# One token tile at a time behind the recurrent block, and half of the sparse queries moved into the first gather phase

## The reference, cut to what matters

```python
h = h + gated @ w_out                                   # recurrent block's output projection, 1024x1024
xt = rms_norm(h, norm_ffn)                              # per token
q = (xt @ w_q).reshape(T, 8, 2, 128)                    # w_q is 1024x2048: two halves of 1024 columns
s = einsum('thpd,hpnd->thpn', q, sub_keys)              # 16 score rows of 128 keys per token
sv, si = top_k(s, 16)                                   # 16 best keys in each half
cand = sv[:, :, 0, :, None] + sv[:, :, 1, None, :]      # 256 pairs per head, of which the 16 best are kept
eidx = ...                                              # 8 heads x 16 = 128 table rows per token
act = gelu(einsum('cd,ckd->ck', xc, u_tab[eidx]))
out = einsum('ck,ckd->cd', gates * act, v_tab[eidx])    # weighted sum of 128 rows of v per token
```

## Time and profile before

| | us |
|---|---|
| median of 3 runs | 2870.07 (2867.79 to 2871.93) |
| the profiled execution | 2877.28 |
| its span | 2875.3 |
| PE busy | 2555.7 (89%) |
| DVE busy | 1343.3 (47%) |
| ACT busy | 651.8 (23%) |
| POOL busy | 499.2 (17%) |
| mean DMA rate over the span | 370 GB/s |

### The profile page before, as it was taken

The page is one execution under the profiler, slowest core; times in us unless marked ns, Lnnn a source line. Parts: engine busy times, 40 slices in busy tenths (PEclk is TensorE's granted clock), DMA queues, the critical chain, the costliest instruction groups (busy, mean ns, idle before and its releaser), DMA issues.

```text
span 2875.3 us, 29405 instructions
## 1 busy us (share of the span) xinstructions
PE 2555.7 (89%) x9916; PEld 1276.8 (44%) x9916; DVE 1343.3 (47%) x3589; ACT 651.8 (23%) x1471; POOL 499.2 (17%) x540
## 2 busy tenths in 40 slices
PE   8899999999999998889777789889789789797776
PEld 6654444443443434778333334446334346333332
DVE  2322222212222112343777776675675675677753
ACT  1310010101000011131222233452232542232212
POOL 1000000000000000001333332232422222333330
PEclk9979999999999999999999999999999899998999
DMA  6559999999999997355999999999999999999994
GB/s 209 222 232 404 419 418 417 419 417 419 418 417 418 417 418 282 109 206 196 421 421 421 421 420 379 410 379 406 421 419 417 377 347 393 421 419 421 422 421 177
DMA packets 180496, 1063.16 MB, mean 370 GB/s; under 512 B 18673, under 2 KB 19089, under 8 KB 81969
## 3 DMA queue, kind: packets, MB, share of 16 engines
q0 software_dynamic: 74880, 540.05, 46.0%
q1 hardware_dynamic: 105520, 521.96, 45.5%
HBM read 1059.31 MB, written 2.62 MB: 369 GB/s over the span
## 4 chain that ended last, share of the span: by engine, by line
PE 53%; DMA 24%; DVE 10%; SPq 6%; ACT 5%; issue 2%; POOL 0%; DVEq 0%; ACTq 0%; POOLq 0%
DMA big<-in_uv,small 16%; PE ps L994 15%; PE ps L658 14%; DMA big<-in_w_gate_up 7%; PE ps L511 7%; PE ps L648 3%; SPq L399 3%; PE ps L811 3%; DVE big L1720 3%; SPq L391 3%; PE ps L945 2%; PE ps L693 2%; PE ps L827 1%; ACT L1316 1%; PE ps L586 1%
## 5 line engine op out<-in xcount | busy, mean ns | idle before, releaser
L994 PE MATMUL ps<-big,small 128*128 128x512 f32 x2048 | 997.1, 637 | 226.6 <-ACT small L1321 226.4
L1861 POOL DMA_INDIRECT big<-in_uv,small x512 | 485.8, 949 | 2265.2 <-DVE small L1700 1279.3
L994 PEld LDWEIGHTS ps<-big,small 128*128 128x128 f32 x2048 | 400.4, 202 | 779.6 <-issue 447.4
L658 PE MATMUL ps<-big 128*64 128x512 f32 x3072 | 705.9, 601 | 22.6 <-DMA big<-in_w_gate_up 18.5
L1720 DVE SCALAR_TENSOR_TENSOR big<-big,ps 128x1024 f32<-128x1024 f32 x512 | 612.6, 1217 | 210.7 <-DMA big<-in_uv,small 209.4
L658 PEld LDWEIGHTS ps<-big 128*64 128x64 f32 x3072 | 203.4, 137 | 418.0 <-issue 340.4
L1321 ACT ACTIVATE small<-con,small 128x128 f32<-128x128 f32 x512 | 177.6, 394 | 309.7 <-DVE small L1731 308.0
L1538 DVE COPY big<-ps 128x512 f32<-128x512 f32 x32 | 22.1, 692 | 418.4 <-PE ps L658 418.4
L511 PE MATMUL ps<-hT,ring 128*128 128x256 f32 x768 | 173.6, 387 | 8.8 <-DVE hT L1361 5.7
L1524 DVE TENSOR_TENSOR big<-ps,big 128x256 f32<-128x256 f32 x64 | 27.2, 424 | 310.8 <-PE ps L675 310.8
L1316 ACT ACTIVATE small<-small 128x2 f32<-128x2 f32 x256 | 52.2, 204 | 527.7 <-DVE big L1720 527.1
(11 more groups left out here) (270 smaller groups left out, 1854.5 us busy)
## 6 DMA issues: line engine op xcount, KB each, us to landing
big<-in_w_gate_up SPq DMA_DIRECT2D x256, 1024.0 KB, 19.7
big<-in_w_down SPq DMA_DIRECT2D x128, 1024.0 KB, 23.4
ring<-in_peer_w_q SPq DMA_DIRECT2D x48, 512.0 KB, 8.1
ring<-in_ple_w_gate SPq DMA_DIRECT2D x32, 512.0 KB, 15.0
ring<-in_w_kv SPq DMA_DIRECT2D x22, 512.0 KB, 10.0
ring<-in_w_in SPq DMA_DIRECT2D x16, 512.0 KB, 5.4
ring<-in_a_w_in SPq DMA_DIRECT2D x16, 512.0 KB, 3.7
big<-in_uv,small POOLq DMA_INDIRECT x512, 15.9
```

What stands on the lines that cost most here:

```text
L658: last = pe.matmul(ps[side * CAP:(side + 1) * CAP, bank + b, :], o, w[:, at:at + BANK], start=start, stop=stop, skip_group_check=True)
L994: last = pe.matmul(ps[:, out_bank(f) + z, :], diagonal(k), rows(k)[:, D + z * BANK:D + (z + 1) * BANK], start=(k % PHASE == 0), stop=((k + ...
L1861: pool.indirect_dma_start(out=rows(k), out_offset=None, in_=io[f"uv{n // UNITS}"], in_offset=bass.IndirectOffsetOnAxis(ap=rows_at[:, at:at ...
```

## The change

From the output projection on, the work goes tile by tile (128 tokens), each with its own half of every step.

- `one_tile` replaces `dense` for `a_out`, `wqa` and `wqb`: the same 8 chunks by 8 matmuls, but with 128 token columns, once for tile 0 and once for tile 1. A ring slot is given free (`w_used`) only by tile 1; tile 0's end is told by `tile_done`.
- After tile 0 of `a_out` DVE adds, ACT squares and DVE norms tile 0 while PE multiplies tile 1. PE's sum of squares of a tile (`tile_squares`) is placed behind the third chunk of the following block.
- PE's order is then: `wqa` tile 0, 2 chunks of `wqa` tile 1, scores of tile 0 (heads 0 to 3), tokens of tile 0, the 6 other chunks of `wqa` tile 1, scores of tile 1.
- The second half of the queries (`wqb`, heads 4 to 7) moves into phase 0: one chunk of tile 0 in each of ticks 0 to 7, its queries copied in tick 8, its scores in tick 9; tile 1 in ticks 16 to 23, copied in tick 24, scores in tick 25, kept in tick 26.
- The two key tables leave the weight ring; SP loads them into `scr` and `gatebuf` ahead of the early chunks. The first half's queries of both tiles now fill one gather buffer (the ninth, `asked`), so POOL waits before gather 8 for the first half's scores of both tiles (`scored` 2), and before gather 9 for nothing more. PSUM banks are dealt out anew.

PE before: the end of the recurrent block, the whole stage, and the first ticks of phase 0. L511 is a `dense` chunk, L501 the sum of squares, L968 the scores, L976 the transposed tokens, L994 the ticks' products.

The two key tables moved ahead of the early chunks; the 16 query chunks now stand together. The diff, cut to its core:

```diff
@@ plan @@
-        ("wqa", 8), ("wqb", 2), ("keysa", 1), ("wqc", 6), ("keysb", 1),
+        ("wqa", 8), ("wqb", 8),
@@ buffers and banks @@
+ASK_HERE, ASK_HERE_COPY, ASK_NEXT, ASK_NEXT_COPY = 0, 8, 16, 24
+        keys0 = (scr, gatebuf)
+        def asked(z, tt):
+            return scr if z else big[:, (ROWS - 2) * ROW + tt * D:(ROWS - 2) * ROW + (tt + 1) * D]
+        def ask_bank(z, tt):
+            return ((4, 2), (4, 0))[z][tt]
+        def score_bank(z, tt):
+            return ((0, 4), (4, 0))[z][tt]
...
-            return (2, 0)[f % 2]
+            return (6, 0, 2, 0)[f]
...
-            return (6, 4)[f % 2]
+            return (2, 4, 6, 4)[f]
@@ SP @@
             sync.wait_ge(x_ready, 8)
+            for z in range(2):
+                sync.dma_start(keys0[z], io["sub_keys"][0][:, z * SLOT:(z + 1) * SLOT]).then_inc(keys_loaded, 16)
...
-            dense("wqa", w)
-            for c in range(2):
-                load(first["wqb"] + c, w[c * P:(c + 1) * P, SLOT:2 * SLOT])
-            load(first["keysa"], keys[:, 0:SLOT])
-            for c in range(2, DT):
-                load(first["wqc"] + c - 2, w[c * P:(c + 1) * P, SLOT:2 * SLOT])
-            load(first["keysb"], keys[:, SLOT:2 * SLOT])
+            dense("wqa", io["peer_w_q"][0], 2)
@@ PE @@
-            dense(first["a_out"], msrc, 0, S["gated_ready"], 0)
+            def one_tile(seg, src, tt, bank, cs=range(DT), ready=None, at=0, between=None):
+                for c in cs:
+                    if ready is not None:
+                        pe.wait_ge(ready, at + c + 1)
+                    w = chunk(first[seg] + c)
+                    for e in range(DT):
+                        last = pe.matmul(ps[:, bank + e // 4, (e % 4) * P:(e % 4 + 1) * P], w[:, e * P:(e + 1) * P],
+                                         src(c)[:, tt * P:(tt + 1) * P], start=(c == 0 and e % 4 == 0),
+                                         stop=(c == DT - 1), skip_group_check=True)
+                    if tt:
+                        last.then_inc(w_used, 1)
+                    elif c == DT - 1:
+                        last.then_inc(S["tile_done"], 1)
+                    if between and c == 2:
+                        between()
+            def tile_squares(tt):
+                for b in range(2):
+                    pe.wait_ge(sq_ready, 20 + 2 * tt + b + 1)
+                    for c in range(4 * b, 4 * b + 4):
+                        last = pe.matmul(ps[:, 7 - tt, 0:P], ones, tile(sq5, c)[:, tt * P:(tt + 1) * P],
+                                         start=(c == 0), stop=(c == DT - 1))
+                last.then_inc(ss_done, 1)
+            one_tile("a_out", msrc, 0, 0, ready=S["gated_ready"])
+            one_tile("a_out", msrc, 1, 2, between=lambda: tile_squares(0))
...
-            sum_squares(5)
-            dense(first["wqa"], hsrc, 0, h_ready, 4 * DT)
-            dense(first["wqb"], hsrc, 4, cs=range(0, 2))
-            scores(0)
-            dense(first["wqc"], hsrc, 4, cs=range(2, DT))
-            pe.wait_ge(S["scores_kept"], 2)
-            tokens(0)
-            scores(1)
+            one_tile("wqa", hsrc, 0, ask_bank(0, 0), ready=h_ready, at=4 * DT, between=lambda: tile_squares(1))
+            pe.wait_ge(h_ready, 6 * DT)
+            one_tile("wqa", hsrc, 1, ask_bank(0, 1), cs=range(0, 2))
+            scores(0, 0)
+            tokens(0)
+            one_tile("wqa", hsrc, 1, ask_bank(0, 1), cs=range(2, DT))
+            scores(0, 1)
             for t in range(TICKS):
+                for tt, begin in ((0, ASK_HERE), (1, ASK_NEXT)):
+                    if t == begin and tt == 0:
+                        pe.wait_ge(S["scores_kept"], 2)
+                    if t == begin and tt == 1:
+                        pe.wait_ge(S["idx_ready"], PH // 2)
+                    if begin <= t < begin + DT:
+                        one_tile("wqb", hsrc, tt, ask_bank(1, tt), cs=[t - begin])
+                    if t == begin + DT + 1:
+                        scores(1, tt)
@@ ACT @@
-            squares(5)
-            used_through(act, "wqa", 8)
-            queries(0)
-            keep(0)
-            used_through(act, "wqc", 6)
-            queries(1)
-            keep(1)
+            tile_squares(0)
+            tile_squares(1)
+            queries(0, 0)
+            queries(0, 1)
+            keep(0)
             exps(0)
             exps(1)
...
+                    if f == 0:
+                        for tt, at in ((0, ASK_HERE_COPY), (1, ASK_NEXT_COPY)):
+                            if t == at:
+                                queries(1, tt)
+                        if t == ASK_NEXT_COPY + 2:
+                            keep(1)
@@ DVE @@
-            add_to_x("a_out", 8)
+            for tt in range(TT):
+                if tt:
+                    used_through(dve, "a_out", 8)
+                else:
+                    dve.wait_ge(S["tile_done"], 1)
+                for b in range(2):
+                    dve.tensor_tensor(of_tile(xT, b, tt), ps[:, 2 * tt + b, :].rearrange("p (c t) -> p c t", c=4),
+                                      of_tile(xT, b, tt), ALU.add).then_inc(x_ready, 1)
+                at = slice(T + tt * P, T + (tt + 1) * P)
+                dve.wait_ge(rms_ready, 6 + tt)
+                link(dve.reciprocal(rs[:, at], rs[:, tt * P:(tt + 1) * P]))
+                for c in range(DT):
+                    dve.scalar_tensor_tensor(tile(hT, c)[:, tt * P:(tt + 1) * P], tile(xT, c)[:, tt * P:(tt + 1) * P],
+                                             col("norm_ffn", c), rs[:, at], op0=ALU.mult, op1=ALU.mult)\
+                        .then_inc(h_ready, 1)
...
-            norm(5, [("norm_ffn", 0)])
@@ POOL @@
                     elif k == ROWS - 2:
-                        used_through(pool, "keysa", 1)
-                    elif k == ROWS - 1:
-                        used_through(pool, "keysb", 1)
+                        pool.wait_ge(S["scored"], 2)
```

More of the change, by code:

```diff
@@ L238, in program @@
             "k_copied k_turned k2_ready v2_ready q_copied q_turned q2_ready "
-            "z_done ln_ready spm_ready rc_done arg_ready w_exp a_ready o_done o_ready gain_loaded early_used "
+            "z_done ln_ready spm_ready rc_done arg_ready w_exp a_ready o_done o_ready gain_loaded tile_done scored early_used "
             "out_ready out_stored moe_step gu_used dn_used"
@@ L960, in score_keys, with scores @@
                 last.then_inc(w_used, 1)
[L962 to L971, removed]
+            def scores(z, tt):
+                pe.wait_ge(keys_loaded, 32)
+                pe.wait_ge(S["pq_ready"], 4 * z + 2 * tt + 2)
+                for hp in range(8):
+                    last = pe.matmul(ps[:, score_bank(z, tt) + hp // 4, (hp % 4) * P:(hp % 4 + 1) * P],
+                                     asked(z, tt)[:, hp * P:(hp + 1) * P], keys0[z][:, hp * P:(hp + 1) * P],
+                                     start=True, stop=True)
+                last.then_inc(S["scored"], 1)
             def tokens(tt):
@@ L1290, in chain, with tile_squares, queries @@
                             act.copy(tile(mT, 2 * z + b, BANK), ps[:, B + b, :]).then_inc(S["scores_kept"], 1)
-            def queries(z):
-                for b in range(4):
-                    act.copy(pq[:, (4 * z + b) * BANK:(4 * z + b + 1) * BANK], ps[:, 4 * z + b, :])\
-                        .then_inc(S["pq_ready"], 1)
+            def tile_squares(tt):
+                for b in range(2):
+                    act.wait_ge(x_ready, 16 + 2 * tt + b + 1)
+                    act.activation(of_tile(sq5, b, tt), of_tile(xT, b, tt), ACT.Square).then_inc(sq_ready, 1)
+                act.wait_ge(ss_done, 6 + tt)
+                act.activation(rs[:, tt * P:(tt + 1) * P], ps[:, 7 - tt, 0:P], ACT.Sqrt, scale=1.0 / D, bias=eps[:, :])\
+                    .then_inc(rms_ready, 1)
+            def queries(z, tt):
+                if tt:
+                    used_through(act, ("wqa", "wqb")[z], DT)
+                else:
+                    act.wait_ge(S["tile_done"], z + 2)
+                if z:
+                    act.wait_ge(S["scored"], 2 + tt)
+                for b in range(2):
+                    act.copy(tile(asked(z, tt), b, BANK), ps[:, ask_bank(z, tt) + b, :]).then_inc(S["pq_ready"], 1)
             def keep(z):
-                used_through(act, f"keys{'ab'[z]}", 1)
+                act.wait_ge(S["scored"], 2 * z + 2)
                 for b in range(2):
-                    act.copy(tile(mT, 2 * z + b, BANK), ps[:, 4 * z + 2 + b, :]).then_inc(S["scores_kept"], 1)
+                    act.copy(tile(mT, 2 * z + b, BANK), ps[:, score_bank(z, 1) + b, :]).then_inc(S["scores_kept"], 1)
             def exps(n):
@@ L1663, in best_keys @@
                 if f == 0:
-                    used_through(dve, f"keys{'ab'[hp // 8]}", 1)
-                    src = ps[:, hp // 8 * 4 + hp % 8 // 4, (hp % 4) * P:(hp % 4 + 1) * P]
+                    dve.wait_ge(S["scored"], 2 * (hp // 8) + 1)
```

(1 more changed line is left out.)

8 lines of the change are left out of this document (5 added, 3 removed).

## The result

| | before | changed |
|---|---|---|
| median, us | 2872.64 (6 runs, 2867.79 to 2874.34) | 2857.60 (6 runs, 2851.45 to 2862.96) |
| ratio | | 0.9947, interval 0.9932 to 0.9961 |
| span of the profiled execution, us | 2875.3 | 2855.4 |

15.0 us off, where 15.6 were forecast. The forecast of 2854.5 us was this saving taken off 2870.07; with six runs the median of before is 2872.64, so 2857.60 is 3.1 us over it. The interval of the ratio is 11 to 20 us, so the time alone doesn't confirm the sum to the microsecond; the places in the profile do that better. These places are all given as distances from the start of the output projection, since that start itself moves by a few us between executions of one program.

The account below looks back on a forecast made before the run. The prediction took a full byte stream from the first gathers on as the bound, with PE setting the pace before it. 21.8 us gained less 6.2 gave 15.6 off, 2854.5 us; range 2847 to 2864.

Parts of the forecast that it names:

- What bounds the kernel: From the first gathers to the end, a stream of bytes at about 420 GB/s; before it, PE sets the pace.
- the theory's sum: Whole kernel: worth is the stream's earlier start, less bytes pushed behind it, plus any time the stream runs dry.
- The lead-in, 54.1 us: PE before its first complete scores: 29 units of 1.865 us, first scores and gather 21.8 us earlier.
- The halved width: PE's 128-column chunks: most of the doubled weight loading hides, 1.865 us a unit against 1.74 for exact halving.
- The new waits: Lead-in: each tile's norm is ready before PE needs it, gaps of 1.45 and 2.87 us go, gather 8 doesn't wait.
- The bytes, 6.2 us (5.0 to 7.5): Behind the first gather: five more chunks lie in the full stream, costing 6.2 us at 420 GB/s.
- Phase 0 priced at nothing: Loaded ticks: 5.4 us of PE lateness fits the ten buffers' cover, so costs nothing; up to 7.8 us without cover.
- the chain: Rival in phase 0: DVE, ACT and PE, not bytes, set it; the whole 28 us count, 2842 us; chance 0.05.
- the PE bound: Rival in the sixteen loaded ticks: PE becomes the bound, all 7.8 us lost, 2862 us; chance 0.13.
- the lasting low clock: Rival in ticks 0 to 7: PE stays at 1.2 GHz, 22 us slower, 2892 us; chance 0.03.
- the load of `wqb` caught in the stream: Rival at the first gathers: 8 chunks more wait, 10 us, giving 2864.5 or about 2868 us; chance 0.10 together.
- The rest is moved as a whole.: From phase 1 on: the weight ring is full in both kernels and what bounds the ticks is untouched.

Follow-up runs that it names:

- late_scores: Changed kernel with 96 more MATMUL instructions (10.7 us of PE) in front of tile 0's scores; ratio to before 0.9977, phase 1 at 427.5 us.
- spread_only: Changed kernel with output projection, norm and first half's queries over all 256 tokens again, second half's queries still in the ticks; ratio to before 0.9986.
- one_cover: Changed kernel with one instead of two chunks of tile 1 between tile 0's last chunk and its scores; 2857.21 us, ratio to before 0.9926.
- more_bytes: Changed kernel with five early chunks loaded a second time behind the query chunks, 2.62 MB more; ratio to before 0.9953, phase 1 at 423.4 us.
- lead_in_only: Changed kernel with the second half's queries, tile by tile, put in front of phase 0 instead of in its ticks; ratio to before 0.9960.
- double_ticks: Changed kernel with every product of the second half's query chunks done twice in ticks 0 to 7 and 16 to 23; ratio to before 0.9959.
- again: Changed kernel run once more without any edit; 2857.62 us, ratio to before 0.9940.
- before_again: Kernel before, without edit, profiled in one more execution; phase 1 at 432.4 us after the output projection's start, no ratio given.

## Why the prediction was right, point by point

- **What bounds the kernel.** Right. The first gather was moved by 10.7 us (`late_scores`), 15 (`spread_only`) and -2 (`one_cover`) and left alone in `more_bytes` and `lead_in_only`; phase 1 lies within 2.3 us of the theory's sum in each. The exception is `double_ticks`, where I left the loads for phase 1 out of the stream. The first product, moved by 26 us between `lead_in_only` and the changed kernel, is worth only the dry spell.
- **The lead-in, 54.1 us.** 53.7 and 52.1 measured. This hid an error of reading. I took a unit at 1.865 us, the length of the scores' row over two. That length runs to the end of the last matmul in the pipe. The distance to the next start is what a unit costs: in the earlier trace rows the scores begin at 1332.20, and the same view of before goes on behind them with a query chunk at 1335.77, so 3.57 for two; in the changed kernel the three `wqa` chunks from 1292.36 take 5.36, 1.787 each. 29 x 1.787 = 51.8. The first profile has 1.6 us of low clock on top, which made it look like my sum; that was luck. `again` hasn't, and shows 52.1 to the MAX8. Of the 22.3 us gained at the MAX8 by the first profile the query chunks ahead of the scores give 18.4 (36.3 before, ten half-width ones now), the hidden norm 4.5, the scores 1.8; `a_out` gives 2.4 back, 1.6 of it to the low clock. The row of before behind the scores, from PE in order of time:

```profile
1335.77 20.89 PE L511 MATMUL ps<-hT,ring 128*128 128x256 f32 x96
```

- **The halved width.** Nearly all of the weight load hides: 1.787 for 128 columns against 1.72, half of a wide chunk by the same measure (from 1236.00 to 1239.45 in the profile of before). There is little left to hide it behind: weight loads are now as busy as the matmuls (66.38 and 66.55 of 67.80 us; 75.00 and 85.68 of 90 before), and no run here shows what a further halving would do.
- **The new waits.** Right: no idle row on PE before the scores, gather 8 without a wait.
- **The bytes, 6.2 us (5.0 to 7.5).** 7.3 us given back in the first pair of profiles (22.2 less 14.9), 7.2 by the megabytes. That is the upper end of my range, as if two chunks and not one were still to land when the stream filled; this term was some 1 us too small, and the saving in the lead-in 0.5 too (22.3 at the MAX8, 21.8 forecast). `more_bytes` bears out the price of a chunk, 4.9 to 5.9 us for five. The prediction set the 358 GB/s of the Trainium skill ("DMA: Bandwidth & Descriptors", section Bandwidth) against the rows. In that section it is a core's share when both cores of the memory domain stream, and one core alone is given 425, with which the 420 measured here agree.
- **Phase 0 priced at nothing.** Right in the outcome: the stream stays full. The evidence for it was misread. In the ticks of the earlier trace rows I set PE's 6.87 us against 5.0 for two gathers, and called the rest 7.4 us of absorbed lateness. But each dense step there lets in a chunk for a later one. From 1704 to 1734, in before, the gathers (software queue) and SP's loads (hardware queue) moved, in MB:

```profile
q0 software_dynamic: 1219, 8.84, 70.8%
q1 hardware_dynamic: 1014, 3.70, 30.8%
```

  So a tick needed some 6.25 us of stream, and four ticks asked for about 2.5 us of cover, not 7.4. The same slip, the other way, made ticks 16 to 23 look 0.3 us over the stream. That the cover of ticks 0 to 7 suffices is shown only by `double_ticks`; the prediction was lucky here.
- **Rivals.** All four fell: the chain (`spread_only`, `lead_in_only`), the PE bound (`double_ticks`, and a share of 1.01 in the ticks), the lasting low clock (granted 1.00 from 1360 to 1376), and the load of `wqb` caught in the stream (SP issued its last chunk at 1325.9).
- **"The rest is moved as a whole."** Nearly. Phases 1 to 3 took 1148.4 and 1148.2 us in the two profiles of before and 1144.5 to 1147.6 in the eight others, whose mean is 1146.0. Most of the 5 us by which the two first spans differ beyond phase 1 is thus spread, but some 2 us may belong to what all eight share (the key tables outside the ring, the new banks). That stays open; it is less than the times can tell.

## What to carry to other kernels

When a long full stream of transfers sets the end, ask of an edit ahead of it three things and nothing else: when does the stream start, which loads fall behind its start that were ahead of it, and does it ever run dry. Busy shares and even the start of the compute behind it don't enter, and time moved off the lead-in is worth less than its length, here 15 of 22 us, as long as the buffers that could take the loads ahead are full. Take an engine's price from start to start, not from the length of a merged row, and before you take from a trace that a buffer absorbed some lateness, count everything that the stream carried in that stretch.

## What the runs showed of the hardware that I had not expected

Behind the same idle gap of 3.10 us in front of the output projection the granted clock fell to 0.50 for about 3 us in the first profile of the changed kernel (12 MATMULs in 2 us), and stayed up in `again`; 1.6 us hang on it. Of the seven profiles that start with the half-width chunks five show it (a mean clock of 0.72 to 0.76 in the first 6 us), and of the three with wide chunks (`before`, `before_again`, `spread_only`) none (1.00); whether the width has to do with it stays open. And the times of one program spread by up to 19 us over 10 runs (`double_ticks` 2855.21 to 2873.94, `spread_only` 2861.62 to 2877.19), so that steps of 5 us were told only by the places in the profile.
